# One inference step of a hybrid decoder: sampled-state updates placed behind the evictions and the partial sum on VectorE

## The reference, cut to what matters

```
z = einsum('bsd,de->bse', rms_norm(h, g_pre), w_in)
qa, ka, va, za, qr, kr, vr, zr, ga, gb = split(z)
```

```
R = R * gamma_h + k^T v
y = q R
```

## Time and profile before

| | |
|---|---|
| median of 3 runs | 2989.02 us (2988.73 to 2989.29) |
| profiled execution | 2989.09 us |
| its span | 2987.3 us |
| TensorE busy | 2902.1 us, 97% |
| VectorE busy | 1774.0 us, 59% |
| ScalarE busy | 1145.6 us, 38% |
| POOL busy | 350.2 us, 12% |
| mean granted TensorE clock | 0.986 |

### The profile page before, as it was taken

How to read it: one execution, slowest core, us unless ns; L and a number is a source line. 1 busy time by engine, 2 the same in 40 slices (tenths; PEclk the granted TensorE clock), 3 DMA queues, 4 the chain that set the end, 5 groups by cost and what they waited for, 6 DMA issues and landing times.

```text
span 2987.3 us, 56953 instructions
## 1 busy us (share of the span) xinstructions
PE 2902.1 (97%) x23406; PEld 2851.4 (95%) x23406; DVE 1774.0 (59%) x3159; ACT 1145.6 (38%) x2078; POOL 350.2 (12%) x517
## 2 busy tenths in 40 slices
PE   7999999999999999999999999999999999999898
PEld 7999999999999998899999999999999999999898
DVE  6766766666667657566667667665654433434632
ACT  5444444444444333333333333433443322334332
POOL 2000000000100011211212112110001101001200
PEclk8999999999999999999999999999999999999999
DMA  8475665655656544546546546576658755553442
GB/s 268 134 225 164 190 190 174 205 174 181 202 175 212 171 138 167 190 151 204 176 164 211 165 171 215 173 262 218 234 207 309 253 191 205 210 203 115 155 168 72
DMA packets 377939, 567.12 MB, mean 190 GB/s; under 512 B 16136, under 2 KB 340552, under 8 KB 374472
## 3 DMA queue, kind: packets, MB, share of 16 engines
q1 hardware_dynamic: 336448, 428.32, 41.7%
q0 software_dynamic: 41232, 135.17, 14.7%
HBM read 511.42 MB, written 228.16 MB: 248 GB/s over the span
## 4 chain that ended last, share of the span: by engine, by line
PE 84%; DVE 5%; DVEq 3%; DMA 3%; ACT 2%; issue 1%; ACTq 1%; SPq 0%; POOL 0%; POOLq 0%
PE acc L535 54%; PE acc L547 21%; DVE weights L1328 1%; PE aux L745 1%; PE aux L756 1%; DVEq L1747 1%; PE aux L766 1%; PE aux L822 1%; ACT weights L952 1%; DVE stage_buffers L1700 1%; PE aux L640 1%; DVEq L1427 1%; PE aux L701 0%; PE aux L648 0%; PE aux L775 0%
## 5 line engine op out<-in xcount | busy, mean ns | idle before, releaser
L535 PE MATMUL acc<-moving,weights 128*128 128x260 f32 x12384 | 1583.2, 286 | 30.5 <-DVE sampled L1403 27.3
L535 PEld LDWEIGHTS acc<-moving,weights 128*128 128x128 f32 x12384 | 1525.7, 190 | 39.4 <-DVE weights L1328 30.5
L1328 DVE TENSOR_TENSOR weights<-raw_weights,weights 128x512 fp32r<-128x512 f32 (+1 forms) x1030 | 708.4, 692 | 633.5 <-ACT weights L952 598.3
L952 ACT ACTIVATE weights<-raw_weights 128x512 fp32r<-128x512 f32 (+1 forms) x1030 | 640.5, 626 | 1125.8 <-PE acc L535 459.5
L547 PE MATMUL acc<-moving,weights 128*128 128x260 f32 x5760 | 704.2, 285 | 15.2 <-DVE moving L1892 8.0
L547 PEld LDWEIGHTS acc<-moving,weights 128*128 128x128 f32 x5760 | 699.4, 190 | 16.9 <-DVE moving L1892 9.4
L535 PE MATMUL acc<-combined_moving,weights 128*128 128x260 f32 x3096 | 425.3, 286 | 8.0 <-DVE partial_sums L1436 7.2
L535 PEld LDWEIGHTS acc<-combined_moving,weights 128*128 128x128 f32 x3096 | 389.6, 188 | 14.2 <-DVE weights L1328 7.9
L1403 DVE SCALAR_TENSOR_TENSOR stage_buffers<-acc,partial_sums 128x260 f32<-128x260 f32 x344 | 146.4, 478 | 170.4 <-PE acc L535 170.4
L952 ACT ACTIVATE weights<-combined_weights 128x512 fp32r<-128x512 f32 x172 | 108.1, 629 | 303.8 <-PE acc L535 282.3
L1328 DVE TENSOR_TENSOR weights<-combined_weights,weights 128x512 fp32r<-128x512 f32 x172 | 118.5, 689 | 144.2 <-ACT weights L952 143.1
(11 more groups left out here) (255 smaller groups left out, 1775.9 us busy)
## 6 DMA issues: line engine op xcount, KB each, us to landing
out<-in_cache_win SPq DMA_DIRECT2D x128, 1023.5 KB, 8.6
raw_weights<-in_w_in SPq DMA_DIRECT2D x96, 1024.0 KB, 5.8
raw_weights<-in_w_in SPq DMA_DIRECT2D x160, 512.0 KB, 5.2
out<-in_cache_win SPq DMA_DIRECT2D x32, 1022.0 KB, 9.3
out<-stage_buffers POOLq DMA_DIRECT2D x120, 256.0 KB, 3.0
stage_buffers<-in_cache_win POOLq DMA_DIRECT2D x48, 512.0 KB, 5.6
stage_buffers<-in_state_ret POOLq DMA_DIRECT2D x64, 256.0 KB, 6.0
raw_weights<-in_w_r_out SPq DMA_DIRECT2D x16, 1024.0 KB, 5.7
```

The costliest lines, as they stand in the source:

```text
L535: mm = pe.matmul(acc[:, m, half, 0:HC], W[:, g % AHEAD, wp, kk, :], mov(up, kk), start=(start and kk == 0 and n == 0), stop=(stop and kk = ...
L952: act.activation(W[:, g % AHEAD, 0, 0:src.shape[1]], src, ACT.Copy).then_inc(s_whi, 1)
L1328: dve.tensor_tensor(W[:, g % AHEAD, 1, 0:src.shape[1]], src, W[:, g % AHEAD, 0, 0:src.shape[1]].bitcast(F32), ALU.subtract).then_inc(s_wre ...
```

## The change

VectorE's hook for the first quarter moves from (0, 8) to (1, 0), in heads 1 to 7 and in the gates: it came between the eviction of `acc[0]` and that of `acc[1]`, and now comes behind both, in step 0 of the next pair, between the passes for weights 5 and 6. In the gates quarters 1 to 3 move from step 2 to step 4 of pairs 2, 4 and 6, and the normalising of the sampled read-out from step 2 to step 4 of pair 9: they stood ahead of the partial sum of step 3 and now stand behind it. No other engine's list changes.

```diff
         def state_hooks(h):
-            return {(0, 8): [lambda: sample_states(0, h)], (1, 5): [lambda: sample_ret_y(0, h)],
+            return {(1, 0): [lambda: sample_states(0, h)], (1, 5): [lambda: sample_ret_y(0, h)],
                     (1, 6): [lambda: sample_states(1, h)], (2, 0): [lambda: sample_ret_y(1, h)],
                     (2, 1): [lambda: sample_states(2, h)], (2, 7): [lambda: sample_ret_y(2, h)],
                     (3, 2): [lambda: sample_states(3, h)], (3, 7): [lambda: sample_ret_y(3, h)]}
 
         def gate_state_hooks(h):
-            return {(0, 8): [lambda: sample_states(0, h)], (1, 6): [lambda: sample_ret_y(0, h)],
-                    (2, 2): [lambda: sample_states(1, h)], (2, 10): [lambda: sample_ret_y(1, h)],
-                    (4, 2): [lambda: sample_states(2, h)], (4, 9): [lambda: sample_ret_y(2, h)],
-                    (6, 2): [lambda: sample_states(3, h)], (6, 9): [lambda: sample_ret_y(3, h)]}
+            return {(1, 0): [lambda: sample_states(0, h)], (1, 6): [lambda: sample_ret_y(0, h)],
+                    (2, 4): [lambda: sample_states(1, h)], (2, 10): [lambda: sample_ret_y(1, h)],
+                    (4, 4): [lambda: sample_states(2, h)], (4, 9): [lambda: sample_ret_y(2, h)],
+                    (6, 4): [lambda: sample_states(3, h)], (6, 9): [lambda: sample_ret_y(3, h)]}
...
             if i == 9:
-                mine[2] = [sample_normed_y]
+                mine[4] = [sample_normed_y]
```

## The result

The changed kernel takes 2971.53 us (median of 4 runs, 2968.70 to 2972.28) against 2989.15 us (4 runs) for the kernel before on the same chip: ratio 0.9939, 95% interval 0.9926 to 0.9951, 17.6 us faster. The profiled execution took 2972.28 us with a span of 2970.5. The time lies in the whole range on record, 2950 to 2975, but outside the forecast's own, 2952 to 2964; its sum, 2958.1, was 13.4 us too good.

A forecast was written before the change was run, and what follows sets the result against it. TensorE, busy nearly throughout, was taken as the bound, losing time waiting for VectorE. Gains 25.8 - 2.0 + 8.8 = 32.6, less 1.6 given back, made 31.0 us: 2989.09 to 2958.1 us; own range 2952 to 2964, whole range 2950 to 2975.

The forecast's parts named there:

- Rival 1: Weights' load lands as late as before; heads 3 to 7 lose 12.5 us at line 822: 2970.6 us, chance 0.15.
- Rival 2: TensorE's clock falls after the new wait at line 822: 7 x 1.6 = 11.2 us lost, 2969.3 us, chance 0.11.
- Seven places: Heads 2 to 7 and gate pair 0: first quarter behind both evictions removes waits and slow clock, gaining 25.8 us net.
- Gates: Quarters 2 to 4 and the sampled normalising moved to step 4: line 1436's waits and slow clock go, gaining 8.8 us.
- Head 1: Its 5.9 us wait stays; the block delays normalising of sampled probabilities, costing 2.0 us, bounds 0 and 3.6.
- I give back 1.6: Allowance of 1.6 us for line 745, already waiting in seven places, where later VectorE work can use up as much again.
- The changed order in the heads is like that one: Weights' load issued ahead of the values, as in gate pair 0, lands in 5.6 to 6.5 us, so nothing is lost.
- the 17 packets of the earlier trace: Head 3's late load: SP's queue had 17 packets against POOL's 269, cited against the round-robin rule and rival 1.
- the new wait: TensorE at line 822 before product 4, seven places: 1.45 us each at full clock, bounds 0 and 3.05.
- Full clock behind 2.37 us: Gate pair 9: granted clock 1.00 behind 2.37 us of idleness, the ground for taking the new wait at full clock.

## Why the prediction was right, and where it was not

The sign and the first half of the mechanism held: the eviction waits went and line 822 took their place. The sum failed in what it gave back, in three terms. The time fell inside the range on record only because that range took in rivals 1 and 2 (2970.6 and 2969.3). That it came out near their times is luck: each of them happened in two heads only, and the chain behind line 745 was in neither.

- *Seven places, forecast 25.8*: 26.5 by the traces. The eviction waits and line 1436 went, line 822 took their place at the stated steps, with 8.2 us in seven waits (10.2 forecast).
- *Gates, forecast 8.8, with gate pair 0 12.2*: 8.1 by the traces for the 8.8, and 12.5 measured alone for the 12.2.
- *Head 1, forecast a cost of 2.0*: 4.6, and 4.5 when taken out beside the moved values. The wait was sized well (1.97); the clock behind it, the upper bound of 3.6 in the forecast, is what came near, with 3.0 us of clock.
- *"I give back 1.6"* for line 745: this is the step that failed. Heads 2 to 7 give back 14.9 us: 4.8 at line 745, 7.0 at late loads, 3.0 by the slow clock, and the last two stood in the sum at nothing. At line 745 the forecast followed the moved block on POOL to the stores and the values and stopped there. Two instructions on, the third quarter's states wait for these stores to land, and come behind 1 MB of values; the scaled keys stand behind that quarter on VectorE. The earlier trace rows show the stores, but no row of line 2046 or 1093 was drawn on.
- *"The changed order in the heads is like that one"* (gate pair 0's, landing in 5.6 us), "so nothing is lost": in four of six heads the load took 5.8 to 7.2 us until VectorE began, in heads 2 and 5 it took 8.7 and 10.8. The 5.6 us of the earlier trace rows were one load without an instruction packet behind its issue; gate pair 0 itself, with the order of the changed kernel, took 8.2 to 11.4 us in five other traces that have the packet. Rival 1, at 0.15, happened in two heads, and in all six when the block came 0.6 us earlier. VectorE's waits for weights in step 5 of heads 3 to 7, which were to fall below 3 us, were 1.3 to 7.3. Nor were the 17 packets of the earlier trace rows all due to the order: the load's first packet started 2.8 us after its issue.
- *Rival 2, the slow clock behind the new wait*: in two of seven places. Counting heads 3 to 7 of six kernels whose first wait is 1.2 us and whose second quarter is on time, the stretch from step 4 to step 10 took 15.4 to 15.5 us in 9 of 26 cases and 13.9 in the rest. Full clock behind 2.37 us was one case, not a rule. The same wait in the same gate pair, in the kernel before with only the values moved, had the clock at 0.5 behind it, and twelve matmuls took 2.72 us instead of 1.68:

```profile
2133.95 2.72 PE L535 MATMUL acc<-combined_moving,weights 128*128 128x260 f32 x12 [2.37 <-DVE partial_sums L1436]
```

That most of the give-back comes from the place of the values is shown: moved alone in the changed kernel they return 10.4 of the 14.9 us. That an instruction packet sets off the late loads of heads 2 and 5 is read from the traces; no run moved those packets by themselves. That the slow clock behind line 822 follows from its wait is supported by its absence there in heads 3 to 7 of the two kernels where the read is later, ten places; why it falls behind one such wait and not behind the next stays open.

## What to carry to other kernels

When a block moves, follow every queue it releases past the first transfer: what waits for that transfer to land, who works on it, and what is queued behind that work, until a buffer is free again. Where two transfers meet, write down how many tenths of a microsecond part them, and do not trust an order that holds by 0.9 us: one share in sixteen that is held up by a microsecond or two is enough for the other transfer to get in front of it. With the less urgent transfer moved, the same load took at most 7.4 us. A wait that is taken away uncovers the next floor, so edits that each bring little (a later read) can pay in full after the floor is lowered.

## What the hardware showed that was not expected

- The same load of 1 MB took very different times until VectorE began. With POOL's second store 0.2 us and the values 0.92 us behind its issue, counted over heads 2 to 7 and gate pair 0 of all traces, it took 5.8 to 6.5 us in the 19 places without an instruction packet on q8 in the 2 us behind the issue, and 6.0 to 11.4 in the 21 places with one (0.99 to 1.79 us long). With the values moved behind the states it was 5.8 to 6.2 in 11 places without and 6.8 to 7.4 in 7 with. In the kernel where TensorE reads later, no such packet falls there, and all seven loads took 5.8 to 6.0.
- In all these 58 places 15 of the load's 16 closing packets of 4 bytes had started by 5.5 us after the issue; where the load was late, it was the sixteenth alone, by up to 10.8 us. With both stores ahead of the load and the values 0.31 us behind it, most of the sixteen were late, the fifteenth at 9.1 to 11.2 us, and the load took 10.8 to 13.4.
- Waits of 1.21 to 1.26 us at line 822 in heads 3 to 7 were followed by a clock partly at 1.2 GHz in 9 of 26 places, at about 1.5 us each; waits of 0.86 to 0.89 in head 2, in two of five.
